# Recurrent stage: sixteen modulation slots summed on VectorE by half slots, three dense weight buffers, another placement of the dense work

## The reference

```
sh1, sc1, ga1, sh2, sc2, ga2 = split(silu(c) @ w_mod + b_mod, 6)      # w_mod 2048 x 12288
p = modulate(rms_norm(x, norm_mix), sh1, sc1) @ w_in                  # for latent and context
r, k, v (1024 columns each), low-rank decay and rate inputs = conv3(p[..., :RW_COLS], rw_shift)
step:  sa = S @ (-kk);  S = S * w + sa (kk*a)^T + v k^T;  y = S @ r   # 16 heads of 64, two directions
y = group_norm(yf + yb) + bonus;  y = y * (sigmoid(gd) @ g_up)
mix = [y, p_cb * conv(p_cg * p_cx), fourier(p_ft)] @ w_out
x = x + ga1 * mix;  x = x + ga2 * ffn(modulate(rms_norm(x), sh2, sc2))
```

## Time and profile before

| | us |
|---|---|
| median of three runs | 3798.11 (3797.06 to 3798.51) |
| profiled execution, its own time | 3796.49 |
| its span | 3794.7 |
| TensorE busy | 3625.2 (96%) |
| VectorE busy | 2223.8 (59%) |
| ScalarE busy | 540.4 (14%) |
| GpSimd busy | 105.0 (3%) |

### The profile page before, as it was taken

The page is one execution under the profiler, slowest core; times in us unless marked ns, Lnnn a source line. Parts: engine busy times, 40 slices in busy tenths (PEclk is TensorE's granted clock), DMA queues, the critical chain, the costliest instruction groups (busy, mean ns, idle before and its releaser), DMA issues. The chain is left out here.

```text
span 3794.7 us, 66630 instructions
## 1 busy us (share of the span) xinstructions
PE 3625.2 (96%) x29257; PEld 3082.1 (81%) x29257; DVE 2223.8 (59%) x4298; ACT 540.4 (14%) x1025; POOL 105.0 (3%) x116
## 2 busy tenths in 40 slices
PE   7999999999989999999999999999989999999999
PEld 4466666667767999999999657667767999999999
DVE  3365555555335988889776535555552756654644
ACT  2221122222100000000000222222221100000000
POOL 0000000000000000000000000000001000000000
PEclk9989999999999999999999999999999999999999
DMA  9722333333348687777667354434413666654553
GB/s 318 242 75 77 86 99 91 93 88 106 85 152 289 219 257 253 254 238 233 209 208 239 119 174 147 151 118 149 156 67 112 201 221 205 200 179 153 170 167 128
DMA packets 680355, 637.95 MB, mean 168 GB/s; under 512 B 42093, under 2 KB 670338, under 8 KB 678658
## 3 DMA queue, kind: packets, MB, share of 16 engines
q1 hardware_dynamic: 569408, 561.05, 46.4%
q10 hardware_dynamic: 110658, 72.64, 6.7%
HBM read 627.36 MB, written 6.29 MB: 167 GB/s over the span
## 5 line engine op out<-in xcount | busy, mean ns | idle before, releaser
L1863 PE MATMUL bank<-extra,work 128*128 128x128 f32 x4224 | 478.9, 275 | 0.0
L1863 PEld LDWEIGHTS bank<-extra,work 128*128 128x128 f32 x4224 | 475.2, 192 | 0.0
L649 DVE SCALAR_TENSOR_TENSOR work<-weight_ring,silu_c,work 128x256 f32<-128x256 f32 x1050 | 421.2, 481 | 0.0
L1863 PE MATMUL bank<-work,weight_ring 128*128 128x128 f32 x2816 | 329.0, 278 | 9.2 <-ACT work L1952 8.8
L1863 PEld LDWEIGHTS bank<-work,weight_ring 128*128 128x128 f32 x2816 | 322.8, 194 | 10.7 <-issue 9.9
L2008 DVE TENSOR_TENSOR work<-weight_ring 128x2048 f32<-128x2048 f32 (+1 forms) x76 | 129.3, 1701 | 292.8 <-DMA weight_ring<-in_w_gate_up 156.6
L979 PE MATMUL bank<-work,x_channels 128*128 128x256 f32 (+1 forms) x736 | 248.0, 477 | 6.0 <-ACT work L1349 3.9
L1919 PE MATMUL bank<-work,weight_ring 128*128 128x128 f32 x2112 | 247.2, 275 | 0.0
L1919 PEld LDWEIGHTS bank<-work,weight_ring 128*128 128x128 f32 x2112 | 241.7, 192 | 3.3 <-issue 3.3
L2396 PE MATMUL bank<-work,weight_ring 128*128 128x512 f32 x448 | 205.6, 604 | 1.8 <-PEq L2182 1.8
L979 PEld LDWEIGHTS bank<-work,x_channels 128*128 128x128 f32 x736 | 137.4, 199 | 77.3 <-issue 55.9
(11 more groups left out here) (403 smaller groups left out, 5284.0 us busy)
## 6 DMA issues: line engine op xcount, KB each, us to landing
weight_ring<-in_w_mod SPq DMA_DIRECT2D x80, 2048.0 KB, 9.9
weight_ring<-in_w_gate_up SPq DMA_DIRECT2D x44, 2048.0 KB, 9.7
weight_ring<-in_w_in SPq DMA_DIRECT2D x26, 2048.0 KB, 10.4
weight_ring<-in_w_down SPq DMA_DIRECT2D x32, 1536.0 KB, 6.8
weight_ring<-in_w_gate SPq DMA_DIRECT2D x22, 2048.0 KB, 8.2
weight_ring<-in_w_up SPq DMA_DIRECT2D x22, 2048.0 KB, 11.8
weight_ring<-in_w_down SPq DMA_DIRECT2D x32, 1280.0 KB, 6.2
weight_ring<-in_w_out SPq DMA_DIRECT2D x16, 2048.0 KB, 9.3
```

What stands on the lines that cost most here:

```text
L649: ins = v_.scalar_tensor_tensor(a, w[:, k, :], c, a, ALU.mult, ALU.add)
L1863: last = mm(out[:, m * P:(m + 1) * P], left[p][:, k, m * P:(m + 1) * P], right[p][:, k, :], start=k == 0, stop=k == 7)
```

## The change

The dense list loses its sixteen `mod` jobs. Each slot is now summed on VectorE: 16 multiply-and-add instructions of 128 x 256, each over one k tile, with the silu value as the per-partition scalar, all into one accumulator `mod_acc`; every instruction waits for the one before it. Weights come in half slots (1 MB, eight k tiles) into a single buffer `mod_half` in what was the fourth weight buffer; ScalarE issues each half (`load_half`) once VectorE has used the half before it. Each head pair has four halves on VectorE: after the first masks, after `z_add`, between the two blocks of transition results, and one instruction a step in chain steps 6 to 13. `modsum` now only sums over partitions (TensorE, four matmuls with a column of ones) and stands at the start of the next pair.

The dense ring has three buffers. `fill` no longer takes work beyond the list of the present pair. `FILL["solve"]` goes from 12.0 to 7.0, and a new fill "rows" of 3.0 stands between the second transition block and `read_rows`.

```diff
@@ dense_jobs @@
     for hp in range(NP1):
+        if hp:
+            jobs.append(("modsum", hp - 1))
...
-        for n, job in enumerate(own):
-            jobs.append(job)
...
-            if n < 2:
-                jobs.append(("mod", mods))
-                mods += 1
+        jobs += own
         ends.append(len(jobs))
+    return jobs + [("modsum", NP1 - 1)], ends
...
+MOD_CHAIN = range(6, 14)
-FILL = {"first": 3.0, "value": 7.0, "ahead": 6.0, "solve": 12.0, "gram": 2.5, "between": 3.0, "chain": 1.5, "step": 0.95}
-WBUFS = 4
+FILL = {"first": 3.0, "value": 7.0, "ahead": 6.0, "solve": 7.0, "gram": 2.5, "between": 3.0, "rows": 3.0, "chain": 1.5, "step": 0.95}
+WBUFS = 3
...
+    wbuf = [take("extra", 2048), take("x", 2048), take("x", 2048)]
+    mod_half = take("slot2", 2048).rearrange("p (k c) -> p k c", k=KT // 2)
...
@@ TensorE @@
                     elif kind == "modsum":
+                        W("mod_step", KT * MOD_GROUP * (i + 1))
...
-                    took = next(work, None)
+                    took = next(work, None) if st.dense_done < limit else None
...
+                limit = DENSE_ENDS[hp]
...
                 transitions(hp, 1)
+                fill(FILL["rows"])
                 read_rows(hp)
...
+            fill_upto(len(DENSE), (NP1, "end"))
             centre_and_gate(NP1 - 1)
@@ ScalarE @@
+            def load_half(n):
+                W("mod_step", KT // 2 * n)
+                c0 = (MOD_FIRST + n // 2) * 256
+                act.dma_start(mod_half, st.dram["w_mod"][n % 2 * 1024:n % 2 * 1024 + 1024, c0:c0 + 256].rearrange("(t p) n -> p t n", p=P)
+                              ).then_inc(S("mod_half_in"), 16)
...  (after the copies of x0_out)
+                load_half(4 * hp + 1)
...  (after the copies of w_out)
+                load_half(4 * hp + 2)
...
                 for n in range(14):
                     dense_out(marks[hp, n])
+                    if n == 1:
+                        load_half(4 * hp + 3)
                 dense_out(marks[hp, "end"])
+                if more:
+                    load_half(4 * hp + 4)
@@ VectorE @@
+            def mod_macs(half, steps):
...
+                    if kc == 0:
+                        ins = v_.tensor_scalar(acc, mod_half[:, k, :], x, None, ALU.mult)
+                    else:
+                        W("mod_step", half * (KT // 2) + k)
+                        ins = v_.scalar_tensor_tensor(acc, mod_half[:, k, :], x, acc, ALU.mult, ALU.add)
+                    ins.then_inc(S("mod_step"), 1)
...  (after the four masks of ak_out)
+                if hp:
+                    W("dense_mm", DENSE.index(("modsum", hp - 1)) + 1)
+                mod_macs(4 * hp, whole)
...  (after the four z_add)
+                mod_macs(4 * hp + 1, whole)
...  (after the first block of mn_out)
+                    if tp == 0:
+                        mod_macs(4 * hp + 2, whole)
...  (in the chain, after a step's two L1656)
+                    if n in MOD_CHAIN:
+                        mod_macs(4 * hp + 3, range(n - MOD_CHAIN[0], n - MOD_CHAIN[0] + 1))
```

More of the change, by code:

```diff
@@ L769, in dense_jobs @@
     conv = [(kind, i) for i in range(NCV) for kind in ("cg", "cx", "cb")]
-    jobs, ends, mods = [("k", 1), ("v", 1), ("r", 1)], [], 0
+    jobs, ends = [("k", 1), ("v", 1), ("r", 1)], []
     for hp in range(NP1):
+        if hp:
+            jobs.append(("modsum", hp - 1))
         if hp + 2 < NP1:
@@ L812, in source @@
     kind, i = job
-    made = {"modsum": ("mod", MOD_GROUP * i + MOD_GROUP - 1), "seq": ("ft", i), "head": ("seq", i)}
+    made = {"seq": ("ft", i), "head": ("seq", i)}
     return DENSE.index(made[kind]) + 1 if kind in made else 0
@@ L873, in rwkv @@
     raw = [take("extra", TA), take("extra", TA), take("late", TA)]
-    mod_rows = take("late", MOD_GROUP, 256)
+    mod_acc = take("late", MOD_GROUP, 256)
     conv_u = take("extra", T)
@@ L983, in dense @@
                             yield 0.856 if both else 0.428
[L984 to L994, removed]
-                                if g == 3:
-                                    yield 0.43
                     elif kind == "modsum":
+                        W("mod_step", KT * MOD_GROUP * (i + 1))
                         for x in range(2 * MOD_GROUP):
-                            last = mm(b[:, x:x + 1], mod_rows[:, x // 2, (x % 2) * P:(x % 2 + 1) * P], c("quads"), start=True, stop=True)
+                            last = mm(b[:, x:x + 1], mod_acc[:, x // 2, (x % 2) * P:(x % 2 + 1) * P], c("ones")[:, 0:1], start=True, stop=True)
                         last.then_inc(S("dense_mm"), 1)
@@ L1027, in dense @@
                         yield 0.856
-            work, ahead = dense(), 0.0
+            work, ahead, limit = dense(), 0.0, 3
             st.dense_done = 0
@@ L1336, in dense_out @@
                                scale=st.par[:, tap:tap + 1]).then_inc(S("dense_out"), 1)
-                    elif kind == "mod":
-                        nc.scalar.copy(mod_rows[:, i % MOD_GROUP, :], b[:, 0:256]).then_inc(S("dense_out"), 1)
                     elif kind == "modsum":
@@ L1442, in _ @@
                 nc.scalar.copy(ysb, bank[0][:, 0:T]).then_inc(S("y_out"), 1)
+            dense_out(marks[NP1, "end"])
             squares(NP1 - 1)
@@ L1604, in head_norm @@
                 v_.tensor_tensor(st.yr[:, hp, :], bank[4][:, T:2 * T], yn, ALU.mult).then_inc(S("y_gated"), 1)
+            def mod_macs(half, steps):
+                slot = half // 2
+                acc = mod_acc[:, slot % MOD_GROUP, :]
+                if 0 in steps:
+                    W("mod_half_in", 16 * (half + 1))
+                for k in steps:
+                    kc = half % 2 * (KT // 2) + k
+                    x = st.silu_c[:, kc:kc + 1]
+                    if kc == 0:
[4 more added lines that the diff above has]
+                    ins.then_inc(S("mod_step"), 1)
+            whole = range(KT // 2)
             unit_keys(0)
```

9 lines of the change are left out of this document (2 added, 7 removed).

## The result

The changed kernel takes 3749.87 us, median of four runs (3746.58 to 3751.16), against 3797.91 (3797.06 to 3798.51) of the kernel before on the same chip. The ratio is 0.9872, 95% interval 0.9855 to 0.9889: 48 us, or 1.3%, faster. The prediction was 3778, range 3757 to 3800: right in its sign, and 28 us short, outside its range.

The account below looks back on a forecast made before the run. The stage was taken as TensorE's program plus a few stops. 29.4 + 22.8 + 3.9 − 13.9 − 5.4 − 13.0 − 3.0 − 0.6 = 20.2 us off the profiled 3796.5 gave 3776.3, as a median 3778, range 3757 to 3800.

Parts of the forecast that it names:

- slots off TensorE: Sixteen modulation slots of 1.84 us each leave TensorE: 29.4 us gained.
- old wait of `read_rows`: TensorE's eight waits of `read_rows` for the last transition result go: 22.8 us gained.
- new waits in `solve`: Shorter fill uncovers ScalarE's copies and `z_add`: 1.9 us in six pairs, 2.5 in pair 0, 13.9 us lost.
- wait before the second block: TensorE waits for the first transition results, 0.9 us a pair over six pairs: 5.4 us lost.
- new wait of `read_rows`: Third half slot delays the second transition results: 2.1 us a pair over six, 0.4 for pairs 0 and 7, 13 us lost.
- end of the chain, last `modsum`: Last chain step uncovered, 3 us; last `modsum` ahead of the centring at the stage's end, 0.6 us.
- stops of "issue" in the blocks: TensorE's stops inside the transition blocks, 26.2 us over eight, run beside the new `read_rows` wait, leaving 2.1 of 5.0 us.
- What leaves TensorE counts in full: Work removed from TensorE shortens the stage fully, as long as what remains still covers the waits.
- third half slot: Between the transition results, VectorE and GpSimd instructions alternate: 7.8 us instead of 4.2.
- rival 4: VectorE's added instruction lengthens each of 64 chain steps by up to 0.52 us: 33 us, 3811; chance 0.08.
- Rival 2: Waits wholly covered as ScalarE's copies and `direction` come earlier; 13.9, 5.4 and 3.0 us come back: 3743; chance 0.08.
- Rival 3: First half slot pushes `direction`; the 5.2 us cut from `solve` return in full, 37 us: 3801, no change; chance 0.10.

Follow-up runs that it names:

- traffic: Changed kernel plus 2 MB of needless HBM copying, issued by ScalarE once each pair's first transition block is done: 3773.89 us, ratio 0.994.
- late-load: Kernel before, with ScalarE's eviction after key_gram and next weight loads held back until both transition blocks are done: 3785.71 us, ratio 0.997.
- narrow multiply-adds: Changed kernel with each multiply-and-add cut to 8 of its 256 columns, all waits and loads kept: 3741.84 us, ratio 0.9851 to the kernel before.
- fastest version: Changed kernel with GpSimd waiting, half load moved, SyncE's next-stage loads after the last pair's blocks, solve 8.5, step 0.83: 3720.91 us, ratio 0.98.

## Why the prediction missed by 28 us

By the two traces, in the order of the prediction's sum. The forecast column sums to 20.2, the measured one to the 50.5 us by which the stage is shorter. Rows of busy time are sums over all forms of a line.

| term | forecast | measured |
|---|---|---|
| slots off TensorE | 29.4 | 30.4 |
| old wait of `read_rows` | 22.8 | 22.8 |
| Fourier eviction | 3.9 | 3.9 |
| new waits in `solve` | −13.9 | −10.1 |
| wait before the second block | −5.4 | −3.3 |
| new wait of `read_rows` | −13.0 | −11.2 |
| end of the chain, last `modsum` | −3.6 | 0 |
| wait of `turned` | not seen | −4.9 |
| stops of "issue" in the blocks | not priced | 8.4 |
| `read_rows` and dense matmuls, shorter | not priced | 15.2 |
| other matmuls, longer in sum | not priced | −3.6 |
| rest | 0 | 2.9 |

The terms that I had priced come to 32.5 us where I had 20.2: the new waits and the end of the chain were put 11.3 us too high. With these alone put right the forecast would have been about 3766, inside the range. What took it out of the range are the terms that I left at nothing: two steps failed.

**The first step that failed** is the one on the stops of "issue". I wrote that they "now run beside" the new wait, used them to bring it from 5.0 to 2.1 us a pair, and let their 26.2 us stand unchanged at both ends. I never asked what makes them long. The change sends ScalarE's loads at other times, since the evictions and loads of the dense jobs moved with the fills. Before, five of the eight pairs had a stop of 3.9 to 5.3 us; after, all of pairs 0 to 6 have one of 1.4 to 2.1, and only pair 7 has a long one, of 5.0. That is 8.4 us (26.6 to 18.2, all idle moments for "issue" ahead of the blocks' own matmuls). The stops of "issue" of the whole stage fall by 10.0, from 35.9 to 25.9, and the other 1.6 us stand in the row "rest". The traffic and late-load experiments settle that cause.

**The second, and the larger,** is the clock. "What leaves TensorE counts in full" left the time of all other matmuls as it was. The earlier trace rows show a granted clock of 0.95 over the stage, and I read past it. In the kernel before, the clock fell to its lower level in every pair, in pair 1 within the wait shown above and right behind the stop:

```profile
412.00:424.00 12.00, 9.14 (x83) 6.86 (x73) 5.61 (x17) 0.00 (x0) 0.90 (x1) 0.72 0.42 120
```

The stop of 4.13 us ends at 411.67, and the wait of 2.86 us starts 0.6 us later. From 412.6 to 419.4 the clock is at its lower level, over `read_rows` and a few dense matmuls: one of the 128 records of `read_rows` took 404 ns in the mean, 288 after. In the changed kernel a stop is 1.6 us and the wait, with the fill "rows" between, 1.6 us [timeline of pair 2 above], and pairs 1 to 4 have no time at the lower clock at all. `read_rows` gave back 5.6 us (14.7 to 9.1) and dense work 9.6 (349.2 to 339.6). Dense work spent 27.4 us at the lower level before and 11.7 after; its records of 256 columns followed each other at 485 ns there and at 250 elsewhere, so about 8 of the 9.6 us are the clock's, an estimate from these numbers. The experiment with the new fills on the old kernel shows it with every slot on TensorE: 41.6 us at the lower clock, and 7.0 us less busy time.

Read pair by pair, the lower clock lasted 3.4 us where the stop was 1.3 or 1.5 us (pairs 2 and 4), 6.8 in pair 6 with two stops of 1.5, and 6.8 to 10.2 us where it was 3.9 to 5.3 (pairs 0, 1, 3, 5 and 7), each with the same wait of 2.84 behind it. The late-load experiment shortened only the stops, left the wait of 2.84 us in every pair, and had 65.3 us at the lower clock in its profiled execution, the fastest of six: shorter stops alone take off up to 23.6 of the 48.2 us. How much of the rest is the wait's is open, for the lengths don't decide it by themselves: in the run with narrow multiply-adds stops of 1.6 to 2.0 us, with no wait of `read_rows` behind them, had 3.4 us at the lower clock in five pairs, where like stops of the changed kernel had none in four.

**What was right.** The slots' own price: 1.84 us each forecast, 1.9 measured (30.4 over sixteen). The old wait of `read_rows` replaced by a new one that is the third half slot's, and none in pair 7: 1.6 us in pair 2, where I had 2.1. I had pairs 1 to 6; it stands in 0 to 4 and 6. The third half slot itself: 6.8 us where the forecast was 7.8 and 4.2 without GpSimd; multiply-adds of 1.37 us beside it and 0.49 otherwise, where I had 1.25; three of the eight instructions were held up in pair 2, where I had four. The Trainium skill (SBUF — State Buffer, section "SBUF: two separate sides") states it as a lock between GpSimd and a VectorE instruction with two SBUF inputs; the trace agrees, 1.38 against 0.49 us. L1614 has one SBUF tensor and a per-partition scalar and was held up as well, 1.33 us where its median is 0.35. With GpSimd made to wait, all are at 0.35 and 0.49 again. The chain had room for the multiply-adds, as forecast (rival 4 false: idle before it is 112.8 us), and no dense weight was late.

**What was off in size.** I had put the wait in `solve` before L1172 or L1177, for ScalarE's copies or `z_add`. It stands before the norms of the next pair, for the squares, because the eviction that moved there goes before them in ScalarE's queue: the same cause (the eviction), one instruction earlier than I looked, 1.5 us instead of 1.9 in pairs 1 to 5 and 0.4 in pair 6, and 2.0 in pair 0, where it does stand before L1172. Before the second block it is 0.63 us instead of 0.9. The uncovered end of the chain isn't there. Against that the change added one wait that I missed: `load_half` at the end of a pair is an instruction on ScalarE's queue ahead of the copies of BKt, and costs `turned` 4.9 us in all. Of the half loads I had followed one through ScalarE's queue, and not the one at the end of a pair.

**Rival 2** gives the nearest number, 3743, by a mechanism that isn't what happened: the waits it takes for covered are there, 24.6 us of them. (Rival 3, at 3801, lies outside my range too, by 1 us; I had named only rivals 2 and 4.)

**Still open.** Old fills with the slots moved give −26 us, new fills with the slots kept −28.7, both together −48. But slots merely left out give −13.7, with more time at the lower clock (102.6 us) than before; the granted clock over the span was 0.974 to 0.978 in its executions, against 0.978 and 0.979. Which of its lost covers sets that wasn't separated; nor was what, beside the lengths of stops and waits, decides in which pairs the clock falls.

## What to carry to other kernels

Before a wait is priced, read the granted clock of the stretch and the stops of "issue" beside it: here idle times of 3 to 5 us in and behind the blocks cost more than their length, since matmuls behind them ran at half speed, and a fill that took a wait away gave part of that back. For a stop of "issue" ask what transfers are in flight there and move those, before the code itself is touched. When work goes off the bounding engine, plan its fills again: here the fills alone were worth 28.7 us, the removed work alone 13.7. And every instruction moved to ScalarE, a DMA issue too, delays what stands behind it in its queue.

## What the chip showed that was not expected

- TensorE's stops in the blocks of small matmuls end 1.2 to 1.6 us after a 16 KB piece of its code has landed. Where the piece started late, each time with loads in flight, they lasted 3.2 to 5.6 us; otherwise 1.1 to 2.3. In the fastest version one of 3.2 us is left, in pair 0, with loads going out at 295.7 and 299.6 and the stop ending at 301.2.
- Code shifted by 128 instructions added 9.6 us of stops. What that cost in time is within the spread of the runs.
- A wait of 2.84 us behind a stop of 1.3 to 1.5 us was followed by 3.4 us at the lower clock in pairs 2 and 4 of the kernel before; in pair 6 of the kernel with its slots left out the same wait, with a stop of only 0.2 us ahead of it, was not.
- GpSimd slowed both kinds of VectorE instruction, 0.49 to 1.38 us and 0.35 to 1.33 in pair 2; over the stage the multiply-and-adds had no length between, L1614 0.82 and 1.16 us too.
- A ring one buffer smaller cost 31 us with the slots in it, and had no wait for a weight without them.
